# Norms of a two-block transformer kernel: one ScalarE table set for logarithm and exponential, and the mean square read by VectorE from its bank

## What is computed

```python
def rmsnorm(x, g):
    xf = x.astype(jnp.float32)
    y = xf * lax.rsqrt(jnp.mean(xf * xf, axis=-1, keepdims=True) + NORM_EPS)
    return (y * g.astype(jnp.float32)).astype(x.dtype)
...
        h = modulate(rmsnorm(x, norm1_g[layer]), sh1, sc1)
...
        x = x + g1 * mix
        h2 = modulate(rmsnorm(x, norm2_g[layer]), sh2, sc2)
        x = x + g2 * swiglu(h2, w_ffn_gate[layer], w_ffn_up[layer], w_ffn_down[layer])
...
        x = x + rms_norm(merged @ w_out[l], ln_mix_post[l])
        h = rms_norm(x, ln_ffn_pre[l])
        f = (jax.nn.silu(h @ ffn_w_gate[l]) * (h @ ffn_w_up[l])) @ ffn_w_down[l]
        x = x + rms_norm(f, ln_ffn_post[l])
```

## Time and profile before

| | |
|---|---|
| median of 3 runs | 2992.29 us (2991.16 to 2992.56) |
| the profiled execution: its time, its span | 2989.5 us, 2987.7 us |
| TensorE, VectorE, ScalarE, GpSimd busy | 2833.1, 1306.2, 1203.6, 1217.4 us |
| granted TensorE clock, mean over the span | 0.979 |

### The profile page before, as it was taken

The page is one execution under the profiler, slowest core; times in us unless marked ns, Lnnn a source line. Parts: engine busy times, 40 slices in busy tenths (PEclk is TensorE's granted clock), DMA queues, the critical chain, the costliest instruction groups (busy, mean ns, idle before and its releaser), DMA issues.

```text
span 2987.7 us, 34123 instructions
## 1 busy us (share of the span) xinstructions
PE 2833.1 (95%) x13512; PEld 2238.8 (75%) x13512; DVE 1306.2 (44%) x1679; ACT 1203.6 (40%) x1742; POOL 1217.4 (41%) x555
## 2 busy tenths in 40 slices
PE   7898999899999999999998999979999999899997
PEld 5777777688887776777786888857757868678885
DVE  4767324421112766835316202277777353341123
ACT  4346643342223555433334222255544233432222
POOL 2122233444444563443444444445624434344442
PEclk9999999899999999999999999989999999999999
DMA  6333122232223121222232222222102213222221
GB/s 248 106 138 135 60 92 93 99 106 99 99 98 128 65 71 36 71 85 78 85 120 71 99 96 95 99 92 80 64 29 74 96 65 112 85 92 99 96 95 64
DMA packets 88991, 277.45 MB, mean 93 GB/s; under 512 B 9920, under 2 KB 10240, under 8 KB 88832
## 3 DMA queue, kind: packets, MB, share of 16 engines
q1 hardware_dynamic: 88832, 275.26, 26.3%
HBM read 267.88 MB, written 7.34 MB: 92 GB/s over the span
## 4 chain that ended last, share of the span: by engine, by line
PE 80%; DVE 11%; ACT 6%; issue 1%; DMA 1%; POOL 1%; SPq 0%; ACTq 0%; DVEq 0%; POOLq 0%
PE bank L1490 24%; PE bank L1492 23%; PE bank L1491 23%; PE bank L1733 2%; PE bank L1548 2%; PE bank L1683 1%; PE bank L1695 1%; DVE pageF L2502 1%; DVE pageF L2576 1%; ACT L1778 1%; DVE pageF L2572 1%; DVE pageF L2305 1%; DVE pageR L2370 1%; PE bank L1724 1%; PE bank L1535 1%
## 5 line engine op out<-in xcount | busy, mean ns | idle before, releaser
L2608 POOL TENSOR_TENSOR wlo<-wraw,whi 128x1024 fp32r<-128x1024 f32 x429 | 1046.8, 2443 | 1472.4 <-ACT whi L1760 1472.2
L1490 PE MATMUL bank<-pageR,whi 128*128 128x512 f32 x3552 | 1446.6, 407 | 64.9 <-ACT pageR L1940 27.7
L1492 PE MATMUL bank<-pageR,wlo 128*128 128x512 f32 x3552 | 1382.9, 389 | 0.0
L1491 PE MATMUL bank<-pageR,whi 128*128 128x512 f32 x3552 | 1382.8, 389 | 0.0
L1490 PEld LDWEIGHTS bank<-pageR,whi 128*128 128x128 f32 x3552 | 675.0, 190 | 247.7 <-issue 104.5
L1491 PEld LDWEIGHTS bank<-pageR,whi 128*128 128x128 f32 x3552 | 675.6, 190 | 153.4 <-issue 25.5
L1492 PEld LDWEIGHTS bank<-pageR,wlo 128*128 128x128 f32 x3552 | 673.9, 190 | 140.4
L1760 ACT ACTIVATE whi<-wraw 128x1024 fp32r<-128x1024 f32 x429 | 450.7, 1053 | 404.4 <-PE bank L1492 397.8
L1821 ACT ACTIVATE pageR<-pageF 128x512 fp32r<-128x512 f32 x136 | 85.9, 632 | 454.7 <-DVE pageF L2364 208.1
L2502 DVE SCALAR_TENSOR_TENSOR pageF<-pageF,prm 128x497 f32<-128x497 f32 (+9 forms) x180 | 202.6, 1126 | 2.7
L2617 POOL TENSOR_TENSOR pageR<-pageF,pageR 128x512 fp32r<-128x512 f32 x46 | 66.1, 1451 | 150.3 <-ACT pageR L1821 150.1
(11 more groups left out here) (211 smaller groups left out, 2062.6 us busy)
## 6 DMA issues: line engine op xcount, KB each, us to landing
wraw<-in_wst SPq DMA_DIRECT2D x429, 512.0 KB, 3.4
pageF<-in_wmod SPq DMA_DIRECT2D x96, 256.0 KB, 4.8
pageF<-in_xT SPq DMA_DIRECT2D x16, 256.0 KB, 4.3
pageF<-in_bias SPq DMA_DIRECT2D x16, 256.0 KB, 3.9
kept<-pageF SPq DMA_DIRECT2D x16, 256.0 KB, 5.3
pageF<-kept SPq DMA_DIRECT2D x16, 256.0 KB, 4.1
out_x<-pageF SPq DMA_DIRECT2D x8, 256.0 KB, 2.0
pageF<-in_cT SPq DMA_DIRECT2D x4, 256.0 KB, 7.1
```

The source lines that it names most:

```text
L1490: e.matmul(o, hi, xh, start=first, stop=False)
L1491: e.matmul(o, hi, xl, start=False, stop=False)
L1492: i = e.matmul(o, lo, xh, start=False, stop=last)
L2608: e.tensor_tensor(wlo[:, b % NH, :, :], wraw[:, b % NR, :, :], bc(whi[:, b % NH, :, :]), ALU.subtract).then_inc(*wlod.up(("wlo", b)))
```

## The change

`rstd_act` no longer makes v; `rstd_dve` takes its place with the form that `first_newton` had, with n as an argument: r * r * (-0.5 / n), then (bank + n * eps) * that, then the same third operation. `first_newton` goes, since `rstd_dve` now serves the two first norms too. The bank `qm` is given back after VectorE's second operation ("rv"), not after v. Page v is no longer taken.

A step `log_exp` takes the place of `warm_ln`. It asks for the table set `natural_log_exp_and_others`, which has Ln and Exp, unless a flag says it is loaded. Every step that uses another function clears the flag. `rstd_act` asks as well, ahead of its waits, and `add(..., last=True)` asks ahead of the last square of a norm on which everything waits.

```diff
     def add(self, src, c0, need, scale=1.0, last=False):
         p, i = self.p, self.n
+        if last:
+            p.step("log_exp")
         p.pages.take(("q", self.tag, i))
...
-    def product(self, mat, bks, warm=False):
+    def product(self, mat, bks):
         p, t = self.p, self.tag
-        if warm:
-            p.step("warm_ln")
         bks.take(("qm", t))
...
     def rstd_act(self, n, bks):
         p, t = self.p, self.tag
-        p.pages.take(("v", t))
         p.pages.take(("r", t))
         p.step("rstd_act", t, self.w, 1.0 / n)
-        bks.give(("qm", t), ("v", t))
...
+    def rstd_dve(self, n, bks):
         p, t = self.p, self.tag
         p.pages.take(("rt", t))
-        p.step("rstd_dve", t, self.w)
-        p.pages.give(("v", t), ("rv", t))
+        p.step("rstd_dve", t, self.w, n)
+        bks.give(("qm", t), ("rv", t))
...
+            def log_exp():
+                if loaded[0] != "both":
+                    loaded[0] = "both"
+                    e.preload_act_table_set("natural_log_exp_and_others")
 
             def rstd_act(t, width, scale):
-                x, v, r = bank(("qm", t))[:, 0:width], F(("v", t))[:, 0:width], F(("r", t))[:, 0:width]
+                x, r = bank(("qm", t))[:, 0:width], F(("r", t))[:, 0:width]
+                log_exp()
                 clear(("r", t))
                 w.wait_ge(*when("qm", t))
                 e.activation(r, x, ACT.Ln, scale=scale, bias=col("eps")).then_inc(*fun.up())
                 w.wait_ge(*fun.last())
                 e.activation(r, r, ACT.Exp, scale=-0.5).then_inc(*fun.up(("re", t)))
-                clear(("v", t))
-                e.activation(v, x, ACT.Identity, scale=scale, bias=col("eps")).then_inc(*fun.up(("v", t)))
...
             def tanh_scaled(dst, o, r):
+                loaded[0] = None
                 w.wait_ge(*when("tgs", dst))
...
-            def rstd_dve(t, width):
-                v, r, x = (F((k, t))[:, 0:width] for k in ("v", "r", "rt"))
+            def rstd_dve(t, width, n):
+                r, x = (F((k, t))[:, 0:width] for k in ("r", "rt"))
                 clear(("rt", t))
                 w.wait_ge(*when("re", t))
-                e.tensor_tensor(x, r, r, ALU.mult).then_inc(*vec.up())
+                e.scalar_tensor_tensor(x, r, -0.5 / n, r, ALU.mult, ALU.mult).then_inc(*vec.up())
                 after()
-                w.wait_ge(*when("v", t))
-                e.scalar_tensor_tensor(x, x, -0.5, v, ALU.mult, ALU.mult).then_inc(*vec.up(("rv", t)))
+                e.scalar_tensor_tensor(x, bank(("qm", t))[:, 0:width], n * EPS, x, ALU.add, ALU.mult).then_inc(
+                    *vec.up(("rv", t)))
                 after()
                 e.scalar_tensor_tensor(r, x, 1.5, r, ALU.add, ALU.mult).then_inc(*vec.up(("rr", t)))
```

More of the change, by code:

```diff
@@ L92, in activation, with preload_act_table_set @@
     def activation(self, *a, **k):
+        return self
+    def preload_act_table_set(self, *a):
         return self
@@ L276, in rstd_act, with rstd @@
         p, t = self.p, self.tag
-        p.pages.take(("v", t))
         p.pages.take(("r", t))
         p.step("rstd_act", t, self.w, 1.0 / n)
-        bks.give(("qm", t), ("v", t))
-    def rstd_dve(self):
+    def rstd_dve(self, n, bks):
         p, t = self.p, self.tag
         p.pages.take(("rt", t))
-        p.step("rstd_dve", t, self.w)
-        p.pages.give(("v", t), ("rv", t))
+        p.step("rstd_dve", t, self.w, n)
+        bks.give(("qm", t), ("rv", t))
         p.pages.give(("rt", t), ("rr", t))
         return ("r", t)
-    def rstd(self, n, mat, bks, early=False, warm=False):
-        if not early:
-            self.product(mat, bks, warm)
+    def rstd(self, n, mat, bks):
+        self.product(mat, bks)
         self.rstd_act(n, bks)
-        return self.rstd_dve()
+        return self.rstd_dve(n, bks)
     def rstd_steps(self, n, mat, bks):
@@ L351, in planned @@
         step("x_square", k)
-    step("warm_ln")
+    step("log_exp")
     for k in range(4):
@@ L411, in planned @@
     mod_rows(0)
-    step("first_newton", "x", T)
+    step("rstd_dve", "x", T, 1024)
     mod_columns(0)
     h_in(0)
-    step("first_newton", "ctx", TC)
+    step("rstd_dve", "ctx", TC, 1024)
     for t in ("x", "ctx"):
@@ L835, in norm_x2 @@
     def norm_x2():
-        r = sq.rstd(1024, "ones", sbk, warm=True)
+        r = sq.rstd(1024, "ones", sbk)
         for k in range(9):
@@ L1238, in post_norm @@
         def post_norm(sf, f, done, gain, prev, ver, each):
-            r = sf.rstd(1024, "ones", mb, warm=True)
+            r = sf.rstd(1024, "ones", mb)
             for m in range(8):
@@ L1746, in scalar @@
             w = Hand(e)
+            loaded = [None]
             def clear(name):
@@ L2016, in scalar @@
             mine = {f.__name__: f for f in (
-                silu_c, w_split, square, warm_ln, rstd_act, x_square, first_norms, mod_row, h_in, hc_in, halves, evict, evict_half, evict_turned, evict_z,
+                silu_c, w_split, square, log_exp, rstd_act, x_square, first_norms, mod_row, h_in, hc_in, halves, evict, evict_half, evict_turned, evict_z,
                 to_tokens, gla_gate, gla_gate_ctx, gla_scan, gla_decays, gla_out, soft_exp, na_out, silu_gate, tanh_gate, h2_hi,
@@ L2082, in ctx_square @@
                         *vec.up(("qa", "ctx", k - 2)))
[L2084 to L2094, removed]
             def h_in(k):
```

5 lines of the change are left out of this document (1 added, 4 removed).

## The result

The changed kernel takes **2962.11 us** (median of 4 runs, 2961.14 to 2965.54), the kernel before 2991.75 (4 runs). The ratio is 0.9903, 95% interval 0.9886 to 0.9920: faster by 29.6 us. The forecast was 2961. The total is right, two of its terms are not. The table loads alone win 35.8 us, more than the whole change; the other half (no Identity pass, VectorE reading the bank) costs some 6 us on top of them, and by itself changes nothing. The rest shows this.

A forecast was written before the change was run, and what follows sets the result against it. TensorE, busy 2833.1 of 2987.7 us, was taken as the bound, leaving 155 us of idle time plus clock loss. Terms 8.3 + 2.6 + 5.2 + 3.8 + 11.8 = 31.7 us off the 2992.29 median gave 2961 us, range 2943 to 2979.

The forecast's parts named there:

- Full stops: Five places where everything waits for one norm: earlier Ln and Exp give 1.9 us at two, 1.5 at three, 8.3 together.
- Start and 140 us: One table load on the path at the start and one before a logarithm of the gates go: 2.6 us.
- 200 to 264 us: Norms beside attention: the next weights' split comes earlier, VectorE's 3.6 us wait closes, 1.6 more: 5.2 us, between 3.6 and 9.2.
- TensorE idles under 5 us: Sign that the forecast holds: TensorE's idle time from 200 to 264 us is under 5 us.
- 264 to 345 us: Two Identity waits for a bank go, some transposes wait for a later score's Exp: 3.8 us, between 1.8 and 6.3.
- One of the signs of being wrong: The forecast is wrong if transposes wait for banks by more than 3 us together.
- rival B: The clock comes back too: shorter idle times bring no fall to half clock, gain 47 us, 2945 us; chance 0.15.
- Layers: Second block's two layers: waits before and behind 968.09 give 3.3 us, two later waits 1.3 each; 5.9 per layer, 11.8 both.
- The new loads at nothing: The 19 new loads before a Tanh or a gate run while ScalarE is idle and cost nothing; uncovered, 1.28 us each.
- VectorE reading the bank at nothing: In the norms, a VectorE step with a bank as operand takes 0.692 us, as with a page: no cost.
- Rival A: Outside the full stops something else is late almost as much, so 10.9 us remain: 2981 us; chance 0.18.
- C: Slower: the new loads lie in front of what TensorE waits for, 24.4 us more, 3006 us; chance 0.03.

The follow-up runs named there:

- the repeat: The changed kernel run once more, unaltered, against the kernel before: 2961.76 us, ratio 0.9901.
- tables_only: The changed kernel with the Identity pass, page v and the early return of the bank put back: 2955.46 us, ratio 0.9879 to the kernel before.
- reads_only: The kernel before with its own table loads, only the Identity gone and VectorE reading the bank: 2990.21 us against 2991.22, ratio 0.9998.
- dummy_identity: The changed kernel plus the Identity pass into page v, waited for but not read, bank returned as late as in the changed kernel: 2962.37 us.
- bank_ops: The changed kernel with all three VectorE operations of a norm on the bank, each with one SBUF input: 2956.23 us, ratio 0.9884.
- mixed: tables_only for the first block's 16 norms of queries, keys and gated outputs, bank_ops for all others: 2948.86 us against 2991.57 for the kernel before.

## Why the prediction was right, and where its steps were not

*Full stops, 8.3 us.* Right: 1.5, 2.0, 1.4, 2.2 and 1.4, together 8.5.

*Start and 140 us, 2.6.* The two waits shrank by 1.2 and 1.4 as counted (in the repeat by 0.7 and 1.4). The lead did not follow (-0.3 and -1.0 by TensorE's instructions): 3.4 us more of the first 150 us ran at half clock in both traces, which takes back 1.7, in tables_only 3.4 us less. reads_only, whose instructions up to 200 us are those of before, also loses 2 us there. Nothing in this stretch is told apart from chance.

*200 to 264 us, 5.2.* The idle time fell by 3.6 and 4.6, at the lower end of the 3.6 to 9.2. VectorE's wait of 3.62 us for a page of in_wmod is gone in the first trace and 1.17 in the repeat, and VectorE is busy for 92 and 91% of the stretch behind it, so that it bounds the rest was right. The sign "TensorE idles under 5 us" held in the repeat (4.60), not in the first trace (5.61).

*264 to 345 us, 3.8.* This is the first step that failed. The two Identity waits went, and the ScalarE time for the transposes was counted. The step "the bank of a norm's mean is now given back after VectorE's second step ... I count 3.8 us" gave 3.05 up to 345 us and then took 1.83 back, behind the place where I stopped reading: 1.2 in all, below the 1.8 of the stated bounds. One of the signs of being wrong came true with it: transposes wait 4.0 us together for banks, in both traces, and the sign said 3. The bank's late return costs 6.6 to 6.9 us (tables_only against dummy_identity). It is hidden in the total because the clock came back in the same stretch: 3.4 us at half clock between 264 and 345 us instead of 16.0, which is worth up to 6.3 (in the repeat 6.8, worth up to 4.6). That is a part of rival B, though 3.2 us of idle time are left there.

*Layers, 5.9 each.* The second failure. The load went from the norm ahead of 968.09 as counted, 1.28 us of lead up to VectorE's first operation; then the third operation ran 1.83 us longer, and TensorE waited 4.17 us where it had waited 3.97. "The Identity was already done when the second of them wanted it, so its removal gives nothing" was said of the stops; in the layers its removal moves GpSimd's split, and I named no queue behind it. The term is 3.0 and 1.9 us of idle time in the changed kernel, 4.8 and 3.6 with the collision cured (bank_ops: 12.68 us left of 17.45, 15.99 of 19.54). Part of what then is still missing are the short waits behind 988 us, counted at 2.0 together and worth 0.7 there.

*The new loads at nothing.* Right for the layers. For the four gates of the first block a single load costs nothing where the bank comes back early (tables_only); in the changed kernel only doubling it was tried, and that cost 2.5 us of idle time.

*VectorE reading the bank at nothing.* Right for the operation, 0.691 us median (longest 0.694) against 0.692; the 65 ns more that the Trainium skill gives ("VectorE: DVE Perf Modes", the section on the TRN2 errata) are not there. An operand in the bank even protects it, which the reckoning did not have.

So the terms counted 31.7 us of idle time. The traces show 20.2 and 22.4, and 3.7 and 4.4 us of TensorE's busy time, which I had put at nothing. The medians are 29.6 apart, since the trace of before is of a quick execution. That the median came out 1 us from the forecast is luck, because errors of both signs met: the loads are worth 35.8 us, more than I forecast for everything, and the other half of the change, for which I counted some 5, costs 6 beside them. What was right is that the change wins by the loads that end a wait, and the full stops to 0.2 us. Rival A (10.9 us) is out; C too.

## What to carry to other kernels

A pass that costs nothing on its own engine still sets when a buffer comes free and when the next engine's work starts: before taking it away, list who waits for its buffer and what stands behind it, and time the two halves of such a change apart. Look in the trace for an operation on VectorE that takes 2.5 us where its line's median is 0.7: a GpSimd operation begun just ahead of it is the cause here, and for the norms' operations an operand kept in the bank cured it. Where functions come in pairs, one table set for both is worth most where the pair ends a wait of TensorE.

## What the runs showed of the hardware that was not expected

- GpSimd's split and a VectorE operation with two SBUF inputs exclude each other for the whole length of the one that came first: 2.52 us instead of 0.69 for VectorE, 2.70 instead of 2.34 for GpSimd. With one input in the bank, 0.69 under the same split. A TENSOR_SCALAR with one page as input is caught as well, 2.51 us instead of 0.43. In the trace of the kernel before, the same count gives 134 of 143 operations without a bank operand, and none of 149 with one.
- The wait for the constants at the start differs by 1.4 us between two executions of one kernel (8.14 and 9.51), and half-clock stretches fall elsewhere (108.8 and 112.3 us in all). The total at half clock is lower in the kernels that idle less, but does not follow the idle time among them: 127.2 us at half clock with 154.6 idle before, 99.0 in tables_only and 88.6 in mixed, both with 127.4 idle.
